# A two-layer hybrid decoder trunk on one core: first rows split in 128-column pieces, first products reordered, last update in halves, transposed rows loaded from ScalarE's queue

## The chip, the cores and the metric

The kernel runs on one core of a Trainium2 chip. The metric is the device time of one execution in microseconds, median of three runs.

## What is computed

A trunk of two layers over 256 tokens of width 1024, all in float32. The reference, cut to its frame:

```python
def hybrid_layer(x, ...):
    proj = rms_norm(x, g_attn_pre) @ w_in + b_in          # 1024 -> 2304: q, k, v of two head groups
    mo = rms_norm(moba_attention(mq, mk, mv), g_moba_out)  # 8 heads; 256 tokens are one block: causal
    so = rms_norm(swa_sink_attention(sq, sk, sv, sinks), g_swa_out)  # window 128, 2 kv heads, sinks
    x = x + rms_norm(concatenate([mo, so]) @ w_out, g_attn_post)
    h = rms_norm(x, g_ffn_pre)
    return x + rms_norm((silu(h @ w_gate) * (h @ w_up)) @ w_down, g_ffn_post)   # d_ff 2816
```

Queries and keys are rotated (rope) before attention.

## The kernel before

**Products.** Each float32 operand is split into a rounded part ("h", made by ScalarE as a copy to float32r) and the residual ("l", made by VectorE as a subtraction), and a product is the sum hh + hl + lh of three TensorE products. The first letter is that of the activations, the second that of the weights. Activations are kept transposed in `actT`, 8 pieces (k) of 128 columns for each of the two row tiles t (128 tokens each).

**Weights.** All weights come as blocks of 128 x 2048 (1 MB), 46 a layer, in the order of use. Block 0 holds 8 k-pieces of 256 columns, blocks 1 and 2 the next 512 columns (4 k each), blocks 3 and 4 the next, and so on. SP issues the load of block b into one of three places of `raw` as soon as VectorE has finished w_l of the block three before it (`load_block`, line 315); ScalarE makes w_h (`hi`, line 502), VectorE w_l (`lo`, line 738), in one of four slots that TensorE frees. `after(L, b)` makes the blocks that the use of block b frees a slot for; in layer 0, after(L, 0) to after(L, 4) make blocks 4 to 8.

**Order.** Every engine's instructions stand in a list written out by hand, once for each engine, and wait on semaphores. TensorE multiplies (`multiply`, line 1087) with the attention steps laid between the blocks: `qk` transposes rotated queries and keys, `scores`, `probs_transposed` (line 1127) takes the exponentials back, `values` (line 1177). VectorE does `project` (bias and rstd, then rope: lines 805 to 835), `maxima` (line 854), `normalise`, `scale_o`, `loT` (line 775: the residual of transposed rows). ScalarE does the exponentials (`exps`, line 568), copies from PSUM (`keep_qk`, line 556) and the sums of squares (`sum_x`, line 537); GpSimd turns those into rstd.

**Start.** The first rows are not transposed on the chip. The host gives x transposed, [128, 8 k, 128 tokens] for each t, and the gains transposed, [128, 8]. SP issues, in this order: xT[0], gT, the first half of block 0, xT[1], the second half, blocks 1 and 2, bias, tables, x (lines 333 to 346). VectorE multiplies xT[0] by the gains (`scale_early`, line 758), GpSimd xT[1] (`scale_first`, line 435), in two halves each. ScalarE rounds each half (`hiT_early`, line 518), VectorE subtracts (`loT_early`, line 766). Blocks 0 and 1 are rounded in halves too (`hi_early`, line 511, and `lo_early`, line 749). TensorE waits for GpSimd's masks, runs eight products on them (`warm`, line 1120), whose result nobody reads, then block 0 in four groups, (half 0, t 0), (half 0, t 1), (half 1, t 0), (half 1, t 1), each with all of hh, lh, hl (`first_block`, line 1112), then block 1 by halves in `multiply`.

**End.** The last tile's y is in two banks; ScalarE sums squares, GpSimd makes rstd, VectorE adds in one instruction of 1024 columns (`update_x`, line 904), and SP stores 512 KB (line 388).

## Time and profile before

| | us |
|---|---|
| median of 3 runs (lowest, highest) | 605.18 (604.11, 605.3) |
| profiled execution, time | 606.41 |
| profiled execution, span | 604.6 |
| TensorE busy | 585.8 (97%) |
| VectorE busy | 361.4 (60%) |
| ScalarE busy | 290.4 (48%) |

The profile is one execution; its span runs from the first to the last instruction. "PE" is TensorE's products, "PEld" its weight loads, DVE VectorE, ACT ScalarE, POOL GpSimd, SPq the DMA queue of SyncE. Ends of products are modelled, so that a row of several products is read by the distance of their starts. The page gives the span in 40 slices of 15.1 us, with the TensorE clock that was granted in each, in tenths. Square brackets behind a row tell how long the engine had been idle before it and what released it.

### The profile page before, as it was taken

The page shows a single profiled execution, that of the slowest core. Times are in us where ns is not written, and L with a number is a line of the kernel's source. Part 1 is how long each engine was busy: PE and PEld are TensorE (multiplying, and loading weights), DVE is VectorE, ACT ScalarE, POOL GpSimd, SP SyncE. Part 2 cuts the span into 40 slices and gives each one's busy share as a digit, 9 for nine tenths or more (in the row PEclk, how much of TensorE's full clock was granted, in tenths as well). Part 3 has the DMA queues.
Part 4 walks back from the last instruction along what each step waited for, and adds up shares of the span by engine and source line. Part 5 has one row for each costly group of instructions (what it writes and reads, how often), then busy time and mean ns, then how long its engine had stood idle before and what let it go on. Part 6 is the DMA issues. An engine that isn't in the chain of part 4 may idle for free.

```text
span 604.6 us, 7614 instructions
## 1 busy us (share of the span) xinstructions
PE 585.8 (97%) x2996; PEld 487.4 (81%) x2996; DVE 361.4 (60%) x458; ACT 290.4 (48%) x406; POOL 45.1 (7%) x70
## 2 busy tenths in 40 slices
PE   5999899999999999999999999999999999999995
PEld 3878787888888889888887788778888888898884
DVE  3878874757545545354596987648556446433632
ACT  3656555746354354155364755466644444423520
POOL 3100000420000000000120010025000000000000
PEclk8899999999999999999999999999999999999999
DMA  8854443157655451549355532416565545342701
GB/s 293 324 197 158 157 181 132 65 215 244 220 198 202 149 207 69 209 151 342 125 208 193 192 132 95 179 66 238 188 241 202 209 150 199 139 178 101 277 1 69
DMA packets 18291, 107.26 MB, mean 177 GB/s; under 512 B 2896, under 2 KB 3152, under 8 KB 6608
## 3 DMA queue, kind: packets, MB, share of 16 engines
q1 hardware_dynamic: 18256, 106.78, 48.0%
q8 instruction: 24, 0.39, 0.2%
q14 instruction: 11, 0.09, 0.0%
HBM read 105.72 MB, written 1.05 MB: 177 GB/s over the span
## 4 chain that ended last, share of the span: by engine, by line
PE 79%; DVE 11%; ACT 6%; issue 2%; DMA 1%; SPq 0%; POOLq 0%; POOL 0%; DVEq 0%; ACTq 0%
PE bank L1087 71%; PE bank L1127 4%; DVE w_l L738 4%; ACT work L568 3%; DVE bank L854 3%; PE bank L1177 2%; ACT w_h L502 2%; PE bank L1112 2%; DMA raw<-in_w_blocks 1%; PE bank L1152 1%; DVE actT_l L775 1%; DVE top L854 1%; DVE work L807 1%; ACT actT_h L530 1%; DVE work L829 1%
## 5 line engine op out<-in xcount | busy, mean ns | idle before, releaser
L738 DVE TENSOR_TENSOR w_l<-raw,w_h 128x2048 fp32r<-128x2048 f32 x90 | 205.5, 2290 | 144.3 <-ACT w_h L502 144.2
L502 ACT ACTIVATE w_h<-raw 128x2048 fp32r<-128x2048 f32 x90 | 171.9, 1916 | 138.0 <-PE bank L1087 119.1
L1087 PE MATMUL bank<-w_h,actT_h 128*128 128x512 f32 (+1 forms) x608 | 235.6, 387 | 1.2 <-DVE actT_l L775 1.0
L1087 PE MATMUL bank<-w_h,actT_l 128*128 128x512 f32 (+1 forms) x608 | 228.9, 377 | 0.0
L1087 PE MATMUL bank<-w_l,actT_h 128*128 128x512 f32 (+1 forms) x608 | 228.3, 375 | 0.0
L1087 PEld LDWEIGHTS bank<-w_h,actT_h 128*128 128x128 f32 x608 | 114.6, 188 | 24.2 <-DVE actT_l L775 3.1
L1087 PEld LDWEIGHTS bank<-w_h,actT_l 128*128 128x128 f32 x608 | 114.4, 188 | 21.5
L1087 PEld LDWEIGHTS bank<-w_l,actT_h 128*128 128x128 f32 x608 | 114.8, 189 | 18.4
L1127 PE MATMUL bank<-ident,work 128*128 128x128 f32 x316 | 46.6, 274 | 4.0 <-ACT work L568 3.3
L1087 PE MATMUL bank<-w_h,fT_h 128*128 128x512 f32 x160 | 49.8, 392 | 0.0
L1087 PE MATMUL bank<-w_l,fT_h 128*128 128x512 f32 x160 | 49.4, 390 | 0.0
L1087 PE MATMUL bank<-w_h,fT_l 128*128 128x512 f32 x160 | 49.3, 389 | 0.0
L1127 PEld LDWEIGHTS bank<-ident,work 128*128 128x128 f32 x316 | 37.3, 141 | 13.6 <-ACT work L568 6.5
L568 ACT ACTIVATE work<-bank,neg_max 128x128 f32<-128x128 f32 (+1 forms) x64 | 26.0, 425 | 36.9 <-DVE neg_max L858 36.9
L1087 PEld LDWEIGHTS bank<-w_l,fT_h 128*128 128x128 f32 x160 | 30.0, 188 | 6.4
L1087 PEld LDWEIGHTS bank<-w_h,fT_l 128*128 128x128 f32 x160 | 30.0, 188 | 6.3
L1087 PEld LDWEIGHTS bank<-w_h,fT_h 128*128 128x128 f32 x160 | 29.5, 188 | 5.7
L449 POOL TENSOR_TENSOR norms<-norms,constants 128x1 f32<-128x1 f32 x8 | 6.7, 840 | 346.6 <-ACT work L546 346.6
L775 DVE TENSOR_TENSOR actT_l<-bank,actT_h 128x512 fp32r<-128x512 f32 (+1 forms) x24 | 14.9, 643 | 23.2 <-ACT actT_h L530 23.2
L606 ACT ACTIVATE work<-bank,norms 128x512 f32<-128x512 f32 (+1 forms) x24 | 15.4, 652 | 22.2 <-PE bank L1087 22.2
L530 ACT ACTIVATE actT_h<-bank 128x512 fp32r<-128x512 f32 (+1 forms) x24 | 12.9, 563 | 27.3 <-PE bank L1127 27.0
L897 DVE TENSOR_TENSOR work<-bank,gain_b 128x512 f32<-128x512 f32 x16 | 10.6, 687 | 24.0 <-ACT work L546 24.0
(73 smaller groups left out, 372.3 us busy)
## 6 DMA issues: line engine op xcount, KB each, us to landing
raw<-in_w_blocks SPq DMA_DIRECT2D x91, 1024.0 KB, 4.8
bias<-in_b_in SPq DMA_DIRECT2D x8, 256.0 KB, 6.2
work<-in_x_transposed SPq DMA_DIRECT2D x2, 512.0 KB, 5.9
raw<-in_w_blocks SPq DMA_DIRECT2D x2, 512.0 KB, 8.6
x<-in_x SPq DMA_DIRECT2D x2, 512.0 KB, 11.3
gain_b<-in_g_attn_post SPq DMA_DIRECT2D x2, 512.0 KB, 7.0
bias<-in_g_ffn_pre SPq DMA_DIRECT2D x2, 512.0 KB, 5.5
gain_b<-in_g_ffn_post SPq DMA_DIRECT2D x2, 512.0 KB, 5.7
```

Of the source, the lines that this page charges most:

```text
L502: nc.scalar.activation(w["h"][:, slot(b), :], raw[:, r, :], ACT.Copy).then_inc(hi_ready, 1)
L530: nc.scalar.activation(dst["h"][:, k:k + nk, tokens(t)], bank[b][:, 0:nk * P].rearrange("p (k n) -> p k n", k=nk), ACT.Copy).then_inc(hiT_ ...
L568: last = nc.scalar.activation(probs[:, j, n * keys:(n + 1) * keys], bank[4 + j][:, n * keys:(n + 1) * keys], ACT.Exp, bias=neg_max[:, g, t ...
L606: nc.scalar.activation(silu[t][:, 0:n], bank[b][:, 0:n], ACT.Silu, scale=rstd_x[:, t:t + 1]).then_inc(drained[b], 1)
L738: nc.vector.tensor_tensor(w["l"][:, slot(b), :], raw[:, slot(b, RAW), :], w["h"][:, slot(b), :].bitcast(F32), ALU.subtract).then_inc(lo_re ...
L775: nc.vector.tensor_tensor(dst["l"][:, k:k + nk, tokens(t)], bank[b][:, 0:nk * P].rearrange("p (k n) -> p k n", k=nk), dst["h"][:, k:k + nk ...
L854: ins = nc.vector.tensor_tensor_reduce(own, own, mask, SCALE, sinks[:, j, head:head + 1] if g == SWA else NEG, ALU.add, ALU.max, top[:, j, ...
L897: nc.vector.tensor_tensor(y[t][:, c, :], bank[b][:], gain_b[:, c * BANK:(c + 1) * BANK], ALU.mult).then_inc(drained[b], 1)
L1087: ins = nc.tensor.matmul(bank[BANK_OF[name]][:, 0:n], left[s][:, at + k, tokens(t)], right[r][:, k, c * BANK:c * BANK + n], start=first an ...
L1112: ins = nc.tensor.matmul(bank[BANK_OF[name]][:, 0:n], actT[s][:, k, tokens(t)], right[r][:, k, :], start=k == 0 and (s, r) == ("h", "h"), ...
L1127: ins = nc.tensor.transpose(out_[:, q * P:(q + 1) * P], src(q), ident[:])
L1177: ins = nc.tensor.matmul(bank[b][:, h * HEAD:(h + 1) * HEAD], probsT[:, j, at:at + P], v[g][:, kb, cols], start=kb == 0, stop=kb == blocks ...
```

## The change

It has eight parts.

1. The transposed rows are loaded by two DMAs on ScalarE's queue; the gains are put in front of the first rows by the host, 1032 columns in one DMA. SP's queue starts with the first half of block 0.
2. The rows are no longer multiplied by the gains beforehand. ScalarE rounds 128 columns at a time with the gain as its scale, VectorE multiplies and subtracts in one instruction of 128 columns. VectorE's, GpSimd's and the halved instructions for them go.
3. ScalarE and VectorE take the first half of block 0 before the second half of the first rows; block 1 is made in one piece instead of two.
4. TensorE runs 16 warming products instead of 8, on a zero tile that VectorE clears, before GpSimd's constants are waited for.
5. TensorE's first products have a new order; in block 1 hh of both tiles, then lh, then hl.
6. In layer 0, ScalarE makes w_h of block 6 before the first exponentials, and VectorE makes w_l of block 7 after `maxima(SWA, 2)` instead of before `project(3, 0)`.
7. In layer 1, VectorE does the residual of the second rows before `project(1, 0)`.
8. The last update is two instructions of 512 columns, each followed by its own store of 256 KB.

The diff, cut to its core (of the old code only what has no counterpart is left out, its functions being described above):

```diff
         y = [work[:, 0:2, :], work[:, 4:6, :]]
...
-        gT = sb("gT", [P, D // P])
+        work_row = work[:].rearrange("p a n -> p (a n)")
+        xT_row = [work_row[:, 4 * BANK - D // P:4 * BANK + D], work_row[:, 4 * BANK + D:4 * BANK + 2 * D]]
...
+        gT = work_row[:, 4 * BANK - D // P:4 * BANK]
+        still = work[:, 9, :].bitcast(BF16)
...
-            sp.dma_start(xT[0], xT_in[0]).then_inc(xT_in_done[0], 16)
-            sp.dma_start(gT[:], gT_in).then_inc(gT_in_done, 16)
             load_first(0)
-            sp.dma_start(xT[1], xT_in[1]).then_inc(xT_in_done[1], 16)
             load_first(1)
...
+            sp.wait_ge(x_ready, X_READY.done(depth - 1, (1, 0)))
+            sp.dma_start(out[0, tokens(0), :], x[:, 0, :]).then_inc(out_done, 16)
+            for c in range(2):
+                sp.wait_ge(half_ready, c + 1)
+                cols = slice(c * BANK, (c + 1) * BANK)
+                sp.dma_start(out[0, tokens(1), cols], x[:, 1, cols]).then_inc(out_done, 16)
...
-            pool.wait_ge(gT_in_done, 16)
-            pool.wait_ge(xT_in_done[1], 16)
-            scale_first(1)
...
-                act.wait_ge(xT_scaled[t], half + 1)
-                k = slice(4 * half, 4 * half + 4)
-                nc.scalar.activation(actT["h"][:, k, tokens(t)], xT[t][:, k, :], ACT.Copy).then_inc(hiT_first[t], 1)
+                if half == 0:
+                    act.wait_ge(xT_in_done[t], 16)
+                for k in range(4 * half, 4 * half + 4):
+                    nc.scalar.activation(actT["h"][:, k, tokens(t)], xT[t][:, k, :], ACT.Copy, scale=gT[:, k:k + 1]
+                                         ).then_inc(hiT_first[t], 1)
...
+            nc.scalar.dma_start(xT_row[0], xT_first_in).then_inc(xT_in_done[0], 16)
+            nc.scalar.dma_start(xT_row[1], xT_second_in).then_inc(xT_in_done[1], 16)
             hiT_early(0, 0)
+            hi_early(0)
             hiT_early(0, 1)
-            hi_early(0, 0)
             hiT_early(1, 0)
-            hi_early(0, 1)
+            hi_early(1)
             hiT_early(1, 1)
-            hi_early(1, 0)
-            hi_early(1, 1)
+            hi(0, 1, wait=False)
             hi(0, 2, wait=False)
...
                     after(L, 1)
+                    after(L, 2)
...
                 keep_probsT(L, SWA, 0)
-                if L == 0:
-                    after(L, 2)
                 after(L, 3)
...
+                for k in range(4 * half, 4 * half + 4):
+                    dve.wait_ge(hiT_first[t], k + 1)
+                    nc.vector.scalar_tensor_tensor(actT["l"][:, k, tokens(t)], xT[t][:, k, :], gT[:, k:k + 1],
+                                                   actT["h"][:, k, tokens(t)].bitcast(F32), ALU.mult, ALU.subtract
+                                                   ).then_inc(loT_first[t], 1)
...
+                for c in range(2):
+                    cols = slice(c * BANK, (c + 1) * BANK)
+                    nc.vector.scalar_tensor_tensor(x[:, 1, cols], y[1][:, c, :], rstd_y[:, 1:2], x[:, 1, cols],
+                                                   ALU.mult, ALU.add).then_inc(half_ready, 1)
...
-            scale_early(0)
+            nc.vector.memset(still, 0.0).then_inc(still_ready, 1)
+            dve.wait_ge(xT_in_done[0], 16)
             loT_early(0, 0)
+            lo_early(0)
             loT_early(0, 1)
-            lo_early(0, 0)
+            dve.wait_ge(xT_in_done[1], 16)
             loT_early(1, 0)
-            lo_early(0, 1)
+            lo_early(1)
             loT_early(1, 1)
-            lo_early(1, 0)
-            lo_early(1, 1)
+            lo(0, 1)
             lo(0, 2)
...
                     lo(L, 3)
-                    project(L, 1, 0)
                     loT(L, ("ht", 0, 1, 0))
                     loT(L, ("ht", 0, 1, 1))
+                    project(L, 1, 0)
                     project(L, 0, 1)
...
                 project(L, 2, 1)
-                after(L, 3)
+                if L:
+                    after(L, 3)
                 project(L, 3, 0)
                 maxima(L, SWA, 2)
+                if L == 0:
+                    after(L, 3)
                 scale_o(L, SWA, 0)
...
+            def early(b, t, half, *parts, last=False):
...
+                for s, r in parts:
+                    pe.wait_ge(lo_half if r == "l" and (b, half) == (0, 0) else
+                               hi_half if (b, half) == (0, 0) else
+                               lo_ready if r == "l" else hi_ready, 1 if (b, half) == (0, 0) else b + 1)
+                    for k in ks:
...
+                        pe.wait_ge((loT_first if s == "l" else hiT_first)[t], k + 1)
...
+                pe.wait_ge(still_ready, 1)
                 for _ in range(n):
-                    nc.tensor.matmul(bank[5][:], masks[:, 1, :], masks[:].rearrange("p a n -> p (a n)"),
-                                     start=True, stop=True)
+                    nc.tensor.matmul(bank[5][:], still[:, 0:P], still[:, P:P + BANK], start=True, stop=True)
...
+            warm(16)
+            early(0, 0, 0, hh, lh, hl)
+            early(0, 1, 0, hh, hl, lh)
+            early(0, 0, 1, hh, lh)
+            early(0, 0, 1, hl, last=True).then_inc(full[BANK_OF["proj", 0, 0]], 1)
+            early(0, 1, 1, hh, hl)
+            early(0, 1, 1, lh, last=True).then_inc(full[BANK_OF["proj", 0, 1]], 1)
+            early(1, 0, 0, hh)
+            early(1, 1, 0, hh)
+            early(1, 0, 0, lh)
+            early(1, 1, 0, lh)
+            early(1, 0, 0, hl)
+            early(1, 1, 0, hl).then_inc(block_used, 1)
+            USED.tick(1)
             pe.wait_ge(const_ready, 8)
-            warm(8)
-            for half in range(2):
-                for t in range(T):
-                    first_block(t, half)
             for L in range(depth):
                 if L == 0:
-                    for half in range(2):
-                        for t in range(T):
-                            multiply(L, t, 1, (half,))
                     multiply(L, 0, 2)
```

## Rows read from the trace of the kernel before

**Rows 1.** The page: TensorE's busy time, share, products; its clock in 40 slices.
```profile
PE 585.8 (97%) x2996; PEld 487.4 (81%) x2996; DVE 361.4 (60%) x458; ACT 290.4 (48%) x406; POOL 45.1 (7%) x70
PEclk8899999999999999999999999999999999999999
```

**Rows 2.** Waits of TensorE over the span: for whom, us in total, times, longest.
```profile
PE bank L1127 <- ACT work L568: 3.3, 6, 1.4
...
PE bank L1087 <- DVE actT_l L775: 1.0, 1, 1.0
```

**Rows 3.** Chain of the work that ended last, 0 to 34 us: start, us, what.
```profile
0.74 0.38 SPq L335
...
1.65 7.78 DMA raw<-in_w_blocks
...
9.45 1.06 ACT w_h L511
...
13.43 6.85 PE bank L1112 x36
20.28 13.63 PE bank L1087 x60
```

**Rows 4.** Stretches: busy and count by engine, granted clock, DMA share, GB/s.
```profile
12.00:18.00 6.00, 5.68 (x25) 5.42 (x26) 4.54 (x5) 4.96 (x6) 1.67 (x2) 0.50 1.01 383
18.00:21.00 3.00, 3.00 (x21) 2.87 (x20) 2.42 (x2) 2.88 (x4) 0.93 (x1) 0.89 0.98 365
```

**Rows 5.** Timeline, 4 to 35 us: start, us, engine, line, what [idle before, releaser].
```profile
4.12 1.42 DVE L758 TENSOR_TENSOR work<-work,gT 128x512 f32<-128x512 f32 x2 [4.12 <-DMA gT<-in_g_first_transposed]
...
4.89 1.32 ACT L518 ACTIVATE actT_h<-work 128x512 fp32r<-128x512 f32 x2 [2.87 <-DVE work L758]
...
5.06 3.54 PE L1120 MATMUL bank<-masks 128*128 128x512 bf16 x8 [5.06 <-POOL masks L419]
...
10.65 0.71 PE L1112 MATMUL bank<-w_h,actT_h 128*128 128x256 f32 x4 [2.05 <-ACT w_h L511]
...
18.85 1.05 ACT L537 ACTIVATE work<-x 128x1024 bf16<-128x1024 f32 x1
...
22.06 0.35 DVE L805 SCALAR_TENSOR_TENSOR v_swa<-bank,norms,bias 128x128 f32<-128x128 f32 x1 [0.79 <-POOL norms L443]
...
25.25 2.28 DVE L738 TENSOR_TENSOR w_l<-raw,w_h 128x2048 fp32r<-128x2048 f32 x1
...
34.06 0.28 ACT L556 ACTIVATE kT<-bank 128x128 f32<-128x128 f32 x1 [5.91 <-PE bank L1127]
```

**Rows 6.** Timeline at layer 0's first maxima and exponentials.
```profile
37.73 0.36 DVE L854 CUSTOM_DVE_ANT_0 bank<-bank,masks,sinks 128x128 f32<-128x128 f32 x1 [4.10 <-PE bank L1152]
...
40.29 0.37 ACT L568 ACTIVATE work<-bank,neg_max 128x128 f32<-128x128 f32 x1 [2.75 <-DVE neg_max L858]
```

**Rows 7.** Timeline of layer 0, w_l of block 7 and TensorE at the third exponentials.
```profile
57.76 2.28 DVE L738 TENSOR_TENSOR w_l<-raw,w_h 128x2048 fp32r<-128x2048 f32 x1
...
65.98 0.63 PE L1127 MATMUL bank<-ident,work 128*128 128x128 f32 x4 [1.43 <-ACT work L568]
66.90 0.30 PE L1127 MATMUL bank<-ident,work 128*128 128x128 f32 x1 [0.28 <-ACT work L568]
```

**Rows 8.** Timeline of layer 1, second rows.
```profile
316.48 0.75 DVE L807 SCALAR_TENSOR_TENSOR work<-bank,norms,bias 128x512 f32<-128x512 f32 x1
...
319.27 1.28 DVE L775 TENSOR_TENSOR actT_l<-bank,actT_h 128x512 fp32r<-128x512 f32 x2
...
320.65 0.36 PE L1087 MATMUL bank<-w_h,actT_h 128*128 128x256 f32 x1 [1.02 <-DVE actT_l L775]
```

**Rows 9.** Timeline of the tail.
```profile
600.28 1.28 DVE L904 SCALAR_TENSOR_TENSOR x<-work,norms,x 128x1024 f32<-128x1024 f32 x1 [0.34 <-POOL norms L452]
601.59 0.34 SPq L388 DMA_DIRECT2D out<-x  x1
```

## What the change does to the time, predicted

> **What bounds the kernel now.** I read the profile page: engine shares, then slices. TensorE is busy 97% of the span of 604.6 us, and only the first two slices have its clock below full [rows 1]. So the reader should look for TensorE's dead time and for the stretch at the low clock. TensorE's own waits, totalled over the span, hold few entries behind the first products: 3.3 us on the exponentials (ScalarE) and 1.0 on actT_l (VectorE) [rows 2]. The change touches the start, three of these waits, and the tail.
>
> The chain of the start [rows 3]: the first half of weight block 0 lands 7.78 us after its issue, at 9.43; ScalarE rounds it in 1.06; TensorE's products of block 0 (line 1112, 48 of them) run to 20.28, and from there on it is fed, 60 products of 512 columns in 13.63 us, 0.2275 each. The 48 have half as many columns, 0.114 each by that row, 5.5 us in all; they take 9.6, from 10.65 on [rows 5], because the granted clock is 0.50 (the 1.2 GHz level) from 12 to 18 us and back near full by 21 [rows 4]. Ahead of the fall TensorE had idled 2.05 us between its eight warming products, 3.54 us from 5.06, and the first real one [rows 5].
>
> **The start: when blocks 0 and 1 can be done.** The warming products no longer wait for GpSimd's masks (5.06) but for a zero tile that VectorE clears. No memset of VectorE is in this trace; a pass of its own over 512 columns is 0.71 (two in 1.42 [rows 5]), and with that they start by 1.5 us. Eight took 3.54, 0.44 each, so sixteen end at 8.5 at the low clock and at 6.5 if it rises half way. They cover the wait for weights and cost nothing on the path; if the weights came first, they would cost what is left of them, 1 us at most.
> The transposed rows leave SP's queue: raw's first half is issued at 0.74, not 1.65 [rows 3]. ScalarE issues the rows instead, two DMAs of 0.38 if priced as SP's [rows 3], beside or ahead of its table load; it did nothing for data until 4.89 [rows 5], so both are covered. When does the half land? At the latest as now, 9.4. At the soonest like the first rows, which with the gains were there at 4.12 [rows 5], plus 1.4 for 512 KB of rows that share the way (383 GB/s [rows 4]): 5.5. I take 7.0, nearer to the soonest, because only 1.4 of the 7.78 us is transfer, and it was issued behind two others.
> What the rows show is that the half lands 5 us behind rows issued 0.9 sooner. The Trainium skill, "DMA: Bandwidth & Descriptors" (Issuing engines are not separate DMA queues), says that DMAs of several engines run on the same 16 DMA engines and that a second issuer saves only issue time. It speaks against this edit: by it the half would land 0.9 us sooner, near 8.5; the sum would stay, as it goes by the cap below, and rival A would grow.
> Pieces: VectorE's scalar_tensor_tensor of 128 columns takes 0.35 [rows 5], so 16 need at most 5.6 us, against four subtractions and two multiplications of 0.71, 4.3: between 0 (they overlap) and +1.3. ScalarE's two halves take 1.32, a copy of 128 columns 0.28 [rows 5]: 16 need 4.5 against 2.6, +1.9, of which half lies ahead of the weights. With the half at 7.0, ScalarE has w_h's half at 8.1, the second rows rounded by 10.3, the rest of block 0 by 11.4 and block 1, two halves of 1.06 [rows 3] from about 14, at 16. VectorE follows by 2.3 for a block (2.28 [rows 5]): block 1's residual at 18.4. TensorE: block 0 needs 5.5 us of full clock and is fed from 8.3 to 14.5; block 1's 16 products that need no residual of w start at 16 and last 3.6, its other 8 last 1.8: done at 21.4, where it is done at 20.28 + 24 x 0.2275 = 25.7 now. 4.3 us sooner.
> **What that is worth.** Behind it stands block 3. Its w_l ends at 27.53, behind two projections on VectorE that begin at 22.06, when rstd is there, 3.2 us after ScalarE's sum_x began at 18.85, when x had landed [rows 5]. Nothing of that chain is edited; it moves only with the backlog of DMAs. TensorE reaches block 3 at 20.28 + 48 x 0.2275 = 31.2 now. So the lead is capped at 31.2 - 27.5 = 3.7 us plus what the backlog gains, at least 0 and at most 1.5 (the first rows had latency and transfer in 3.4 us, 0.74 to 4.12 [rows 3, 5]; with 1.4 of sharing, 3.0 of the 7.78 are stall, and half of it could go). I take 0.3: 4.0 us; bounds at full clock 3.5 and 5.0.
> Later feeding moves along with the lead: VectorE had waited 4.10 us for the scores at 37.73 and ScalarE 2.75 for the maxima at 40.29 [rows 6]. Hoisting after(0, 2) puts one rounding of 1.9 us into the latter wait; behind it are queued the first exponentials, for which TensorE waits. The cover is 0.8 us; each us beyond it costs one.
>
> **Layer 0, w_l of block 7 behind the maxima.** Its 2.28 us at 57.76 stand in VectorE's run ahead of the maxima; TensorE waits 1.43 at 65.98 and 0.28 at 66.90 for the exponentials that need them [rows 7]. Taken out, the maxima come 2.28 sooner, more than the 1.71, and what is late next is TensorE's own order. The moved instruction ends when VectorE's next step began before, so nobody behind it is later; the next raw load, which waits for it, goes out 4.7 us later (60.04 to about 64.8), between 0 and 1 us. I take 1.6 of the 1.71.
> **Layer 1, loT ahead of project(1, 0).** TensorE waits 1.02 at 320.65 for actT_l, whose two halves (1.28) run from 319.27, behind a projection that began at 316.48 [rows 8]. Swapped, loT is through by 318, TensorE wants it at 319.6: the wait goes, and the projection, ending 1.3 later at 320.6, is wanted by a transpose behind six products of 0.2275 and eight shorter. 1.0.
> **Tail.** Now one update of 1.28 and one DMA of 512 KB, from 601.59 to the end at 604.63 [rows 9]. In halves: two updates of 0.7, one DMA beside the second, and the last moves 256 KB: 0.7 less at 383 GB/s, 0.15 more to compute. Bounds 0 and 0.7; 0.5.
>
> **The sum:** 4.0 + 1.6 + 1.0 + 0.5 = 7.1 us. On the profiled execution: span 604.6 to 597.5, time 606.4 to 599.3. The median of the runs, 605.18, lies 1.2 below the profiled one: 598.1.
>
> **Rivals.**
> Low clock at the start (A). If the half lands late, TensorE idles over 2 us behind the warming products, as it did ahead of the fall [rows 4, 5]; a second pause stands ahead of block 1 (14.5 to 16). Against it: the pause of 1.43 at 65.98 lies in slices whose clock is full [rows 1, 7]. If it falls as now, for some 7 us, half of them, 3.4, is lost; 1.0 of that is slack ahead of block 3, so the lead is 1.6: 600.5. Here a rule speaks for the forecast: the Trainium skill, "TensorE: Matmul & The Clock Gate" (What's actually happening and its table), has the clock fall only after a whole idle window. The fall in [rows 4] came with 2.05 us of idling, so I go by the row.
> The reorders return nothing (B): from 66 us on VectorE and ScalarE pace the attention steps, TensorE's waits there are small [rows 2], and what is won ahead of it is lost there: without the 1.6 and 0.5 of the lead, 600.2.
> The backlog gains more (C): 5.0 or over, 597.1 and below.
> It does not do what it says (D): weights as late as now and the clock down, so only layer 1 and the tail pay: 603.7.
> Slower (E): the clock stays at 1.2 GHz through block 1, because TensorE now runs small groups released piece by piece, as from 12 to 18 us, where its busy time of 5.68 in 6.00 [rows 4] did not lift it. The three blocks up to block 3 are 16.4 us of work at full clock from 8.3 on; low until T, they end at 8.3 + 16.4 + (T - 8.3)/2. Low until block 1 is done, T = 30, block 3 is reached at 35.6 instead of 31.2: 4.4 us lost against 3.1 won elsewhere, 606.5. It decides from T = 27.5.
>
> **How the numbers follow.** Forecast 0.54 (597.1 to 599.4), A 0.17, B 0.13, C 0.08, D 0.05, E 0.03. The range 596.0 to 602.0 leaves out D, E and part of C and of A, 0.15. A measurement of this kernel can tell about 0.2%, 1.2 us: faster by more holds in all but E and part of D, 0.93; same 0.04; slower 0.03.
>
> **What would show it.** Right: the first L511 between 5.5 and 8, block 1's last product near 21.4, w_l of block 3 ending near 27 and TensorE on block 3 right behind; no wait of TensorE on ScalarE near 62 and on L775 near 312; a last DMA of 256 KB 2.4 us before the end; granted clock 1.00 from 8 us on. Wrong: a clock of 0.50 behind 8 us (A, E), the first exponentials late behind the hoisted rounding, new waits between 62 and 105 us (B), or the half at 9 us again.

## The result and the profile after

| | us |
|---|---|
| before, median of 5 runs beside the changed kernel (lowest, highest) | 604.11 (602.63, 605.3) |
| after, median of 5 (lowest, highest) | 598.48 (598.25, 598.82) |
| ratio, with its 95% interval | 0.9907 [0.9886, 0.9928] |
| profiled execution of after: time, span | 598.48, 596.7 |

The changed kernel is 5.6 us faster by the medians. Between the two profiled executions the distance is larger, 604.6 to 596.7, 7.9 us. That difference is the main thing to be explained.

The page of after, its sections 1 and 2: busy time of TensorE, and the clock in 40 slices. [rows 1] show the low slices at the start, which are gone.

```profile
PE 585.4 (98%) x3004; PEld 486.1 (81%) x3004; DVE 362.0 (61%) x469; ACT 292.8 (49%) x417; POOL 42.1 (7%) x68
...
PEclk9999999999999999999999999999999999999999
```

The waits of TensorE over the whole span of after (us in total, times, longest):

```profile
PE bank L1108 <- ACT w_h L500: 1.6, 1, 1.6
PE bank L1123 <- ACT work L559: 1.5, 4, 0.8
PE bank L1117 <- DVE work L912: 1.5, 1, 1.5
PE bank L1123 <- ACT kT L547: 0.5, 1, 0.5
```

Against [rows 2] the wait on the exponentials fell from 3.3 to 1.5, the 1.0 on actT_l is gone, and the wait for w_h between the warming products and the first real one is 1.6 where it was 2.1.

The chain of waits of after in its first 36 us (start, us, what), from the DMA to the feeding of blocks 0 to 3:

```profile
0.74 6.18 DMA work<-in_x_first_transposed
6.94 1.28 ACT actT_h L508 x4
8.22 0.96 ACT w_h L500
9.22 1.22 PE bank L1108 x8
10.48 10.94 PE bank L1108 x64
21.42 8.16 PE bank L1083 x36
```

Compare [rows 3]. The chain no longer begins with the weights but with the first rows, which land 6.18 us after their issue; ScalarE's four pieces (0.32 each) come next, and only then the first half of block 0, which had landed by then: 6.0 us after its issue at 0.74. TensorE is fed without a gap from 10.48.

The timeline of after, rows of TensorE, ScalarE and VectorE (start, us, engine, line, operation; idle time before it and its releaser in brackets):

```profile
1.45 6.17 PE L1117 MATMUL bank<-work 128*128 128x512 bf16 x16 [1.45 <-DVE work L912]
...
8.13 1.04 ACT L500 ACTIVATE w_h<-raw 128x1024 fp32r<-128x1024 f32 x1
...
9.22 0.74 PE L1108 MATMUL bank<-w_h,actT_h 128*128 128x256 f32 x4 [1.60 <-ACT w_h L500]
...
15.79 2.00 PE L1108 MATMUL bank<-w_h,actT_h 128*128 128x512 f32 x8
...
24.04 2.29 DVE L729 TENSOR_TENSOR w_l<-raw,w_h 128x2048 fp32r<-128x2048 f32 x1
```

And its windows of the same stretches as [rows 4] (busy time of each engine, granted clock, DMA share, GB/s): the clock is 1.00 where it was 0.50 and 0.89.

```profile
12.00:18.00 6.00, 6.00 (x42) 5.55 (x41) 5.30 (x10) 5.26 (x7) 0.00 (x0) 1.00 1.03 327
18.00:21.00 3.00, 3.00 (x15) 2.49 (x14) 2.23 (x2) 2.31 (x4) 1.13 (x3) 1.00 0.85 338
```

The end of after in its timeline, beside [rows 9]: the last piece of 512 columns begins at 593.44, its store is issued at 594.21, and the span ends 2.5 us later, at 596.7.

```profile
593.44 0.75 DVE L897 SCALAR_TENSOR_TENSOR x<-work,norms,x 128x512 f32<-128x512 f32 x1
594.21 0.33 SPq L391 DMA_DIRECT2D out<-x  x1
```

**Where the 7.9 us lie.** A mark that both profiles have is the first transpose of `qk(0, 0)`, behind block 3: it begins at 33.75 before and at 29.43 after, 4.3 us for the start. From there to the seam of the layers the two profiles differ by 1.95 (layer 0's reorder), in layer 1 by 1.26, from the last product on by 0.43 (tail). Together 7.96. For layer 1 the timeline of after has the residual of the rows, which ended the wait in [rows 8], already at 310.71, ahead of the projection that stood before it:

```profile
310.71 1.29 DVE L756 TENSOR_TENSOR actT_l<-bank,actT_h 128x512 fp32r<-128x512 f32 x2 [0.40 <-ACT actT_h L521]
311.91 0.74 DVE L788 SCALAR_TENSOR_TENSOR work<-bank,norms,bias 128x512 f32<-128x512 f32 x1
```

### The profile page after: what moved, and what is told of

Its sections match the earlier page's. It is cut to its first block, busy times and chain, and to the rows that moved or that the text cites. A ratio compares the mean times of both kernels' runs of the same rounds, so it can differ in the third digit from the quotient of the medians.

```text
span 596.7 us, 7657 instructions
## 1 busy us (share of the span) xinstructions
PE 585.4 (98%) x3004; PEld 486.1 (81%) x3004; DVE 362.0 (61%) x469; ACT 292.8 (49%) x417; POOL 42.1 (7%) x68
## 4 chain that ended last, share of the span: by engine, by line
PE 85%; DVE 6%; ACT 6%; DMA 1%; issue 1%; DVEq 0%; POOLq 0%; POOL 0%; ACTq 0%
PE bank L1083 75%; PE bank L1123 4%; ACT work L559 3%; DVE w_l L729 3%; PE bank L1173 2%; DVE bank L835 2%; PE bank L1108 2%; ACT w_h L494 2%; PE bank L1148 1%; DMA work<-in_x_first_transposed 1%; DVE actT_l L756 1%; DVE top L835 0%; ACT actT_h L521 0%; ACT work L575 0%; DVE neg_max L839 0%
## 5 line engine op out<-in xcount | busy, mean ns | idle before, releaser
L729 DVE TENSOR_TENSOR w_l<-raw,w_h 128x2048 fp32r<-128x2048 f32 x91 | 207.7, 2290 | 144.2 <-ACT w_h L494 144.1
L494 ACT ACTIVATE w_h<-raw 128x2048 fp32r<-128x2048 f32 x91 | 173.9, 1917 | 143.0 <-PE bank L1083 118.1
L1083 PE MATMUL bank<-w_h,actT_h 128*128 128x512 f32 (+1 forms) x600 | 232.3, 387 | 0.2
L1083 PE MATMUL bank<-w_h,actT_l 128*128 128x512 f32 (+1 forms) x600 | 225.9, 377 | 0.0
L1083 PE MATMUL bank<-w_l,actT_h 128*128 128x512 f32 (+1 forms) x600 | 225.2, 375 | 0.0
L1083 PEld LDWEIGHTS bank<-w_h,actT_h 128*128 128x128 f32 x600 | 113.1, 189 | 22.6 <-issue 2.7
L1083 PEld LDWEIGHTS bank<-w_h,actT_l 128*128 128x128 f32 x600 | 112.9, 188 | 21.2
L1083 PEld LDWEIGHTS bank<-w_l,actT_h 128*128 128x128 f32 x600 | 113.2, 189 | 18.3
```

What stands on the lines that cost most here:

```text
L494: nc.scalar.activation(w["h"][:, slot(b), :], raw[:, r, :], ACT.Copy).then_inc(hi_ready, 1)
L729: nc.vector.tensor_tensor(w["l"][:, slot(b), :], raw[:, slot(b, RAW), :], w["h"][:, slot(b), :].bitcast(F32), ALU.subtract).then_inc(lo_re ...
L1083: ins = nc.tensor.matmul(bank[BANK_OF[name]][:, 0:n], left[s][:, at + k, tokens(t)], right[r][:, k, c * BANK:c * BANK + n], start=first an ...
```

## The experiments

The theory was that every part pays as in the sum of the prediction. The rivals to be told apart: whether the start gives its 4.0 us in the usual execution or only against the profiled one, and which of its edits gives it: warming, clock, queue, pieces, order of products, or the gains that stop having a DMA of their own. The batches ran on several chips, and the kernel before, repeated beside each, had medians of 603.76 (18 runs), 605.31 (12), 605.56 (10) and 605.5 (11), with single runs from 601.76 to 606.34. So each ratio is taken against the runs beside it. Where two medians of different batches are compared below, that is said. Kernels whose start does not vary agree across the batches to 0.2 us (598.45, 598.57, 598.6), so the chips themselves hardly differ; it is the start of before that does. "Mark" below is the start of that first transpose in the profile of the kernel.

**1. Parts 6 to 8 alone** (`b_678`: the kernel before with only the reorders and the tail)

```diff
+                    after(L, 2)
                 ...
-                if L == 0:
-                    after(L, 2)
...
-                    project(L, 1, 0)
                     loT(L, ("ht", 0, 1, 0))
                     loT(L, ("ht", 0, 1, 1))
+                    project(L, 1, 0)
```

> The kernel before with parts 6, 7 and 8 alone: w_h of block 6 and w_l of block 7 moved in layer 0, the second rows' residual ahead of project(1, 0) in layer 1, the last update and store in halves. Start as before. My sum gives 1.6 + 1.0 + 0.5 = 3.1 us. If the attention stage eats the reorders (rival B): 1.5 us. In the trace: no wait of TensorE of 1.43 near 64 us and none of 1.02 near 319 us. Theory 'the first lead makes them larger' (they pay only with TensorE ahead): under 2.5 us here, against the 3.4 that the two profiles differ by behind 34 us.

600.03 (598.74 to 601.85, 7 runs) against 603.76: 3.7 us, ratio 0.9937 [0.9913, 0.996]. Its start is unedited, and yet its profile has the mark at 29.73, not 33.75, and a full clock: in this execution the first half of the weights landed 5.7 us after its issue at 1.64, not 7.78. Its timeline, the first w_h:

```profile
7.34 1.06 ACT L515 ACTIVATE w_h<-raw 128x1024 fp32r<-128x1024 f32 x1 [0.98 <-DMA raw<-in_w_blocks]
```

So the start of [rows 3 to 5] is not what the unchanged code always does. It is one outcome of several, and this profile is one too: with 598.74 it is of the fastest of the seven runs.

The mean granted clock, which is on record for each single run, tells how often. Before's profile, with its fall of some 7 us, has 0.992. Of the 51 runs of before in these batches 16 have 0.992 or 0.993, with a median of 606.0 us; 12 have 0.994 or 0.995 (605.5 us); 23 have 0.996 or more (603.8 us). The share differs by batch: 5 of 18 runs at 0.995 or below where the median was 603.76, and 23 of 33 in the other three.

**2. Parts 1 to 5 alone** (`a_no678`: after with 6, 7 and 8 put back)

> The changed kernel with parts 6, 7 and 8 undone: only the start is changed (rows on ScalarE's queue, pieces, order, warming). Theory 'luck' (the start of before varies from execution to execution by where the weights land and whether the clock falls; the profiled one was a slow one, so the start is worth less on the median than the 4.3 us between the two profiles): the median gains 1.5 to 2 us over before, though its profile reaches the first transposes near 29.4 us. Theory 'sum' (my 4.0 us for the start): the median gains 4 us.

601.96 (601.69 to 603.56, 7 runs), ratio 0.9954 [0.9935, 0.9973]: 3.5 us slower than after, so parts 6 to 8 are worth 3.7 added and 3.5 taken away. The waits of TensorE in this kernel show the two terms coming back, 2.9 for 1.5 on the exponentials and the 1.0 on actT_l:

```profile
PE bank L1104 <- ACT work L555: 2.9, 7, 0.8
...
PE bank L1064 <- DVE actT_l L753: 1.0, 1, 1.0
```

What is left for the start is 600.03 - 598.48 = 1.5 us by the medians of two batches on top of parts 6 to 8 (1.6 within the batch of `b_678`, against `a_sp_rows` of experiment 5). By the runs beside this kernel it is more: 605.31 - 601.96 = 3.4 by the medians, 2.8 by the ratio (0.46%), which has an interval of 1.6 to 3.9. The batches differ in how often before has its slow start, and the worth of the start with them.

**3. The clock alone** (`b_warm34`: before, with 34 warming products on a zero tile in place of 8)

```diff
+            warm(34)
             pe.wait_ge(const_ready, 8)
-            warm(8)
```

> The kernel before with one edit: 34 warming products on a zero tile cleared by VectorE instead of 8 on the masks, so that TensorE is busy up to about 10.5 us; rows, pieces, order and queues stay as they were. Theory 'clock' (most of what the start gained is that TensorE's clock no longer falls; the earlier rows and weights and the new order bring little): granted clock 1.00 throughout, block 2 is started near 21.5 (bound by w_l of block 2, which ended at 21.3 in before) instead of 25.6, block 3 near 27.5, and the time falls by 3.0 to 3.7 us. Theory 'feeding' (the start gained because rows and weights are ready sooner and are used in a better order): the old order with its waits for whole halves starves TensorE whatever its clock, block 2 starts at 24 or later, gain under 1.5 us.

604.12 (603.43 to 605.67, 12 runs), ratio 1.0002 [0.9987, 1.0018]: nothing on the median. In its profile the clock never fell, though the half again landed 8.0 us after its issue; of its 12 runs two have a mean clock of 0.994 and 0.995. Its timeline, the warming products and the first w_h:

```profile
1.45 10.09 PE L1124 MATMUL bank<-work 128*128 128x512 bf16 x34 [1.45 <-DVE work L922]
...
9.62 1.06 ACT L513 ACTIVATE w_h<-raw 128x1024 fp32r<-128x1024 f32 x1 [3.26 <-DMA raw<-in_w_blocks]
```

And its window, with a clock of 1.00 where [rows 4] have 0.50:

```profile
12.00:18.00 6.00, 5.24 (x43) 4.86 (x41) 4.38 (x5) 4.85 (x6) 1.83 (x2) 1.00 1.03 376
```

Between its profile and that of before the mark moved from 33.75 to 31.99: between these two executions, a clock that stays up is worth 1.8 us. The run tells less about the median than meant, because 34 were too many: the first real product began at 11.19, 0.5 us after its weights were ready at 10.68. In an execution with the early half, as in the profile of `b_678` (weights ready at 8.40), the same warming would stand in the way for 2.8 us, by an estimate from these two rows.

**4. Half the warming in the changed kernel** (`a_warm8`: `warm(8)` for `warm(16)`)

> The changed kernel with 8 warming products instead of 16 (nothing else). They end near 5 us, TensorE idles 4 us until the first weights at 9.2. Theory 'clock': the granted clock falls to 0.50 from some point before 12 us, block 0 and part of block 1 run at half speed, the time rises by 2 to 4 us over the changed kernel. Theory 'feeding': no more than 0.5 us, since nothing is fed later.

599.56 (598.97 to 599.93, 6 runs), ratio 0.9927: 1.1 us slower than after, and the ranges don't touch. TensorE idled 4.0 us, and the clock fell for a short time (0.50 from 8.7 to 12.1 us). Its timeline, the first real product, and then its window from 6 to 12 us, where the mean clock is 0.72:

```profile
9.06 1.22 PE L1108 MATMUL bank<-w_h,actT_h 128*128 128x256 f32 x4 [4.01 <-ACT w_h L500]
```

```profile
6.00:12.00 6.00, 2.94 (x14) 2.94 (x14) 4.10 (x12) 5.22 (x14) 0.00 (x0) 0.72 1.03 430
```

So the longer warming is worth about 1 us here on the median. In the profile it is less: the mark is at 29.87 for 29.43. That eight are enough where the rows come from SP's queue (experiment 7) suggests that the longer warming only pays for the later landing of the rows; that was not shown by a run of its own.

**5. The rows on SP's queue again** (`a_sp_rows`: after, gains still merged, rows issued by SP in the old order)

```diff
+            sp.dma_start(xT_row[0], xT_first_in).then_inc(xT_in_done[0], 16)
             load_first(0)
+            sp.dma_start(xT_row[1], xT_second_in).then_inc(xT_in_done[1], 16)
             load_first(1)
...
-            nc.scalar.dma_start(xT_row[0], xT_first_in).then_inc(xT_in_done[0], 16)
-            nc.scalar.dma_start(xT_row[1], xT_second_in).then_inc(xT_in_done[1], 16)
```

> The changed kernel with the two loads of transposed rows back on SP's queue in the old order (rows, first half of block 0, second rows, second half), nothing on ScalarE's queue. If the second queue matters: the first half lands 1 us or more later than in the changed kernel (there before 8.1), ScalarE's first rounding of weights starts later and block 1 ends later; +0.5 to +1.5 us, or more if the longer idling lowers the clock. If a second issuer only saves issue time: rows land sooner (near 4 us), the half near 8.5, no more than 0.5 us either way, since block 3 (VectorE's w_l) caps the lead.

598.45 (597.92 to 599.28, 6 runs), ratio 0.991 [0.9884, 0.9937]: the same as after. The queue is worth nothing. The half of the weights lands 5.9 us after its issue at 1.18, at 7.03, against 6.0 after 0.74 in after: the second issuer saved 0.3 us. The rows now land 3.3 us after their issue, where they took 6.18 on ScalarE's queue, and w_h starts 1.1 us sooner, at 7.05, on the weights. Most of that is lost again at block 3, as [rows 5] had let expect: VectorE's w_l is not done in time, and TensorE waits for it (mark at 28.99, 0.4 sooner than after). Three rows of its timeline:

```profile
7.05 1.06 ACT L502 ACTIVATE w_h<-raw 128x1024 fp32r<-128x1024 f32 x1 [1.76 <-DMA raw<-in_w_blocks]
...
23.79 2.29 DVE L729 TENSOR_TENSOR w_l<-raw,w_h 128x2048 fp32r<-128x2048 f32 x1 [0.25 <-ACT w_h L496]
...
26.13 0.50 PE L1083 MATMUL bank<-w_h,actT_h 128*128 128x512 f32 x1 [0.33 <-DVE w_l L729]
```

**6. Halves for pieces** (`a_halves`: after with the first rows rounded and subtracted in instructions of 512 columns. It leaves out the multiplication of the first rows by the gains)

```diff
-                for k in range(4 * half, 4 * half + 4):
-                    nc.scalar.activation(actT["h"][:, k, tokens(t)], xT[t][:, k, :], ACT.Copy, scale=gT[:, k:k + 1]
-                                         ).then_inc(hiT_first[t], 1)
+                k = slice(4 * half, 4 * half + 4)
+                nc.scalar.activation(actT["h"][:, k, tokens(t)], xT[t][:, k, :], ACT.Copy).then_inc(hiT_first[t], 1)
```

> The changed kernel with the first rows handled in halves of 512 columns (4 instructions on ScalarE and 4 on VectorE instead of 16 and 16). It leaves out the multiplication of the first rows by their gains, since one instruction can take only one gain per partition. Price of the pieces alone: ScalarE spends 2.5 us on them instead of 5.0, VectorE 2.8 instead of 4.5. Theory 'capped' (block 3 and the DMA backlog set the lead): same time within 0.3 us. If the pieces are on the path: 0.5 to 1 us faster.

598.6 (597.81 to 599.01, 6 runs), ratio 0.9897 [0.9875, 0.9919]: the same as after. Here w_h starts at 7.14, 1.0 sooner: 0.65 by the pieces (0.54 us from the first rounding to w_h, for 1.19 in after), the rest because the rows landed 0.3 sooner in this execution. Again TensorE waits at block 3, by the view of its waits:

```profile
PE bank L1082 <- DVE w_l L728: 0.2, 1, 0.2
```

Two kernels whose first products come a microsecond earlier (8.16 and 8.23 against 9.22) have their marks only 0.4 and 0.7 earlier (28.99 and 28.77), and on the median they end together with after: the cap at block 3 holds.

**7. Parts 6 to 8 with the gains merged** (`b_678_merged`: `b_678`, and the gains stand in front of the first rows in one DMA; order, queue, halves, eight warming products and the order of the products as before)

```diff
-            sp.dma_start(xT[0], xT_in[0]).then_inc(xT_in_done[0], 16)
-            sp.dma_start(gT[:], gT_in).then_inc(gT_in_done, 16)
+            sp.dma_start(xT_row[0], xT_first_in).then_inc(xT_in_done[0], 16)
             load_first(0)
-            sp.dma_start(xT[1], xT_in[1]).then_inc(xT_in_done[1], 16)
+            sp.dma_start(xT_row[1], xT_second_in).then_inc(xT_in_done[1], 16)
             load_first(1)
```

> The kernel before with parts 6, 7 and 8 and the gains in front of the first rows in one DMA (of the start nothing else: SP's queue in the old order, two multiplications on VectorE and two on GpSimd, halves, 8 warming products on the masks). Theory 'gains' (the 128 rows of 32 bytes queued ahead of the first half of block 0 stall some of the DMA engines: in the kernels that have that DMA the half took 5.7, 7.3, 7.8 and 8.0 us, in those without it 5.7 to 6.0): the half takes 6 us or less, the median falls from 600.0 to about 599, and the spread shrinks. Theory 'accident' (late landings come from somewhere else): median 599.7 to 600.7, the half at 7 us or more in the profile as likely as not.

598.57 (598.16 to 598.67, 4 runs), ratio 0.9884 [0.9871, 0.9898]. That is the time of after, without the other queue, the pieces, the longer warming and the new order. Against `b_678`, in another batch, the one edit takes 1.5 us by the medians and 3.2 by the two ratios (0.9884 for 0.9937), and the spread goes from 3.1 us (7 runs) to 0.5 (4 runs). The half lands 6.0 us after its issue; the first w_h in the timeline:

```profile
7.17 1.06 ACT L515 ACTIVATE w_h<-raw 128x1024 fp32r<-128x1024 f32 x1 [0.93 <-DMA raw<-in_w_blocks]
```

Its chain of waits runs elsewhere, over the second rows and GpSimd's multiplication of them, and so does that of `b_678` in its profile:

```profile
1.63 6.83 DMA work<-in_x_second_transposed
...
8.63 1.77 POOL work L439
...
11.99 4.10 PE bank L1130 x32
```

From there TensorE is fed, and the mark is at 29.56 (after: 29.43). That chain leaves slack for the first products, which fits with more warming bringing nothing to this start, as the next two runs find.

**8 and 9. Sixteen warming products with either form of the gains** (`b_678_warm16`, `b_678_merged_w16`: on the zero tile, ahead of the wait for the constants)

```diff
+            warm(16)
             pe.wait_ge(const_ready, 8)
-            warm(8)
```

> The kernel before with parts 6, 7 and 8 and the 16 warming products on a zero tile, started by VectorE's clearing; rows, pieces, order and queues as before. If warming is what the start is worth on the median: 598.5 to 599, as the changed kernel, and less spread than b_678 (598.7 to 601.9). If the order and the pieces matter: 599.5 to 600, as b_678 without it (600.03).

> As b_678_merged, and with the 16 warming products on VectorE's zero tile. With the weights sooner the products end less than 2 us ahead of the first real one: the granted clock stays up in every run. If landing and clock together are what the start is worth, 598.5 to 598.8 as the changed kernel. If the new order and the dropped multiplications are worth something of their own, it stays at 599.2 or above.

600.67 (599.31 to 602.6, 6 runs), ratio 0.9932, with the gains apart; 598.68 (598.54 to 599.09, 4 runs), ratio 0.9889, with the gains merged. Warming changes neither (ratios 0.9937 and 0.9884 without it); merging is again worth 2.0 us by the medians and 2.6 by the ratios, in two batches. The first of the two caught a late landing in its profile, 7.3 us after issue, an idle time of 3.46, and the fall of the clock. Its timeline, the first w_h and the first real product, then its window from 12 to 18 us (clock 0.76):

```profile
8.91 1.06 ACT L517 ACTIVATE w_h<-raw 128x1024 fp32r<-128x1024 f32 x1 [2.56 <-DMA raw<-in_w_blocks]
...
10.11 0.71 PE L1134 MATMUL bank<-w_h,actT_h 128*128 128x256 f32 x4 [3.46 <-ACT w_h L517]
```

```profile
12.00:18.00 6.00, 5.56 (x38) 5.30 (x37) 4.95 (x5) 5.49 (x6) 1.12 (x2) 0.76 1.05 357
```

Over the profiles of this study the half lands 7.78, 5.7, 8.0 and 7.3 us after its issue where the gains' DMA stands ahead of it on its queue (before, `b_678`, `b_warm34`, `b_678_warm16`), and 5.9 to 6.0 where it does not (`a_sp_rows`, `b_678_merged`, `b_678_merged_w16`). In the seven profiles in which the half is first on SP's queue it is 5.4 to 6.0. The second rows, which follow the half on that queue, show the same: 8.6, 6.7, 8.7 and 8.1 us with the gains' DMA, 6.7 to 6.9 without.

**10 and 11. The gains apart, behind the rows on ScalarE's queue** (`a_gain_apart`: after, with a DMA of 128 rows of 32 bytes for them; `a_gain_wide`: the same with rows of 512 bytes)

```diff
             nc.scalar.dma_start(xT_row[0], xT_first_in).then_inc(xT_in_done[0], 16)
+            nc.scalar.dma_start(gT, gT_in).then_inc(gT_in_done, 16)
             nc.scalar.dma_start(xT_row[1], xT_second_in).then_inc(xT_in_done[1], 16)
...
                     act.wait_ge(xT_in_done[t], 16)
+                    if t == 0:
+                        act.wait_ge(gT_in_done, 16)
```

> The changed kernel with the gains in a DMA of their own (128 rows of 32 bytes) behind the first rows on ScalarE's queue, nothing else. Theory 'gains': the first half of block 0 or the second rows land 1 to 2 us later in some runs, median 599 to 600, spread over 1 us. Theory 'accident': 598.3 to 598.7, as the changed kernel.

> This is a_gain_apart with one difference: the gains, still in a DMA of their own behind the first rows on ScalarE's queue, come as 128 rows of 512 bytes (64 KB, padded with zeros) instead of 128 rows of 32 bytes (4 KB). Sixteen times as many bytes, and the same number of DMAs in the same order. If it is the rows of 32 bytes that hold up what lies beside them, the delay goes: the time is that of after, 598.5 us (597.9 to 599.2), the first w_h of block 0 starts near 8 us in the profile instead of 10.56, and the granted clock stays up. If it is the further DMA, or the further semaphore that ScalarE and VectorE wait for, whatever its rows are, nothing changes: 602.0 us (601.4 to 602.8), w_h again at 10 us or later. Between them, about 600, would mean that both carry a share.

602.03 (601.72 to 603.01, 5 runs), ratio 0.9943, and 602.99 (602.0 to 603.4, 6 runs), ratio 0.9958. The whole gain of the start is gone in both, and the size of the rows is not the cause. The chain of waits of `a_gain_apart` says what is:

```profile
1.17 6.84 DMA work<-in_g_first_transposed
...
8.09 1.28 ACT L511
...
9.38 1.28 ACT actT_h L511 x4
10.66 0.96 ACT w_h L501
```

The gains land 6.84 us after their issue, although they are 4 KB, and ScalarE can go on at 8.09, where the rows let it begin at 6.94 in after. The 1.28 at 8.09 is ScalarE's table load: with a second wait ahead of the first rounding it stands behind the wait, where in after it lay hidden at 1.66. 1.15 + 1.28 = 2.4 us, and w_h starts at 10.56 for 8.13. TensorE then idles 3.7 us, the clock falls (0.53 from 12 to 18 us), and the mark is at 33.74 for 29.43: 4.3 us, of which 2.4 are the later w_h; the other 1.9 are put down to the clock.

The table load in the timeline of after, and then in that of `a_gain_apart`:

```profile
1.66 1.28 ACT L508 ACT_TABLE_LOAD   x1 [1.66 <-PEq L1371]
```

```profile
8.09 1.28 ACT L511 ACT_TABLE_LOAD   x1 [8.09 <-DMA work<-in_g_first_transposed]
```

The half of the weights itself landed 5.4 and 5.5 us after its issue in the two, so on another queue this DMA does not hold it up. But it does hold up what stands behind it on its own queue, the second rows. Their time from issue to landing in after, `a_gain_apart` and `a_gain_wide`, each from the view of the line that issues them (L601, L605, L606):

```profile
DMA to landing us min/median/max: 8.6/8.6/8.6
DMA to landing us min/median/max: 10.1/10.1/10.1
DMA to landing us min/median/max: 10.3/10.3/10.3
```

In the four other kernels that have both rows on ScalarE's queue without this DMA it is 8.2 to 8.4. Rows of 512 bytes delay them as much as rows of 32, so the small rows are not needed for a delay of this size.

**12. TensorE's own order** (`a_plus`: after, and products moved between dependent steps)

```diff
-                    multiply(L, 0, 3)
+                    multiply(L, 0, 3, (0,))
                     qk(L, 0, 0)
+                    multiply(L, 0, 3, (1,))
...
                     probs_transposed(L, SWA, 0, 0)
-                    probs_transposed(L, SWA, 0, 1)
                     multiply(L, 1, 4, (0,))
+                    probs_transposed(L, SWA, 0, 1)
...
                 probs_transposed(L, MOBA, 2, 0)
-                probs_transposed(L, MOBA, 2, 1)
                 multiply(L, 0, 12, (0,))
+                probs_transposed(L, MOBA, 2, 1)
```

> The changed kernel with TensorE's order edited at the waits that are left: qk(0, 0) of layer 0 between the halves of block 3, half a block between the two probs_transposed of the first round (layer 0) and of the last MOBA round (both layers). The waits there are 0.45, 0.76, 0.28 and 0.28 us. If they are dead time of TensorE alone, 1.7 us less: 596.7. If VectorE or ScalarE pace these stages, the waits appear elsewhere: under 0.8 us.

596.61 (596.44 to 596.97, 5 runs), ratio to before 0.9866 [0.9845, 0.9888], 1.9 us faster than after (2.0 than `a_halves`, the same as after, in its own batch): the fastest kernel here. The 0.5 on kT is gone, and of the 1.5 on the exponentials 0.5 is left, by its waits:

```profile
PE bank L1123 <- ACT work L559: 0.5, 2, 0.3
```

## Why the prediction was right, and where it was not

**The time.** 598.1 was forecast and 598.48 measured, inside the likeliest case. But the gain was 5.6 us, not the 7.1 of the sum: the three runs of before shown ahead of the prediction had a median of 605.18, and with two more beside them it is 604.11. How large the gain is depends on which runs of before one takes. Over all 56 on record before has 605.1, which makes it 6.6; `a_sp_rows`, as fast as after, gains 5.3 in its batch and `b_678_merged` 7.0 in its own. So the time agrees partly by luck: a start valued too high was taken from a median of three that could as well have been 1 us lower.

**The start: 4.0 forecast, 4.3 between the profiles, 1.5 to 3.4 on the medians.** From block 1 on the mechanism inside the profile went as told: block 1's last product at 15.79 + 24 x 0.2275 = 21.25, forecast 21.4; w_l of block 3 done at 26.33, TensorE on block 3 at about 26.7, and no wait between. The first link did not: w_h of the first half began at 8.13 and was done at 9.17, where the sum had it done at 8.1 and the list of signs had it begin between 5.5 and 8. It waited not for the weights but for the first rows, which landed at 6.92 and not near 4 as in before, and for four pieces of them. The slack ahead of block 3 hid that. The cap was tested from the other side by `a_sp_rows` and `a_halves`, which reach it with 0.3 and 0.2 us of waiting. (The bounds told for this term, 3.5 and 5.0, do not come out of its own figures: 3.7 and between 0 and 1.5 more make 3.7 and 5.2.) The step that failed is the one that carried the sum over to the median: "The median of the runs, 605.18, lies 1.2 below the profiled one". It shifts the time by 1.2 and leaves the term of the start at its size in that one execution, an execution with the late half (7.78 us) and the low clock. `b_678` shows that the same code also lands it in 5.7 with the granted clock at 1.00. The late landing and the fall of the clock are outcomes that vary between executions of before. By an estimate from the runs sorted by their clock, with 3.6 us for parts 6 to 8 and 598.5 for after, the start is worth 606.0 - 3.6 - 598.5 = 3.9 us in executions with the low clock of the profile, as forecast, and 603.8 - 3.6 - 598.5 = 1.7 in those with 0.996 or more. A large part of what the change does for the start is to remove that variation: after spreads over 0.6 us, before over 2.7.

**When the half lands.** 7.0 was taken for the time of its landing, and it landed at 6.7; in after it isn't on the chain, the rows are. The argument "only 1.4 of the 7.78 us is transfer, and it was issued behind two others" had the right suspect in its second half, one of the two others: the gains' DMA, if not the reason. But the gain was put down to the queue, and `a_sp_rows` shows that the queue is worth 0. Here the rule of the Trainium skill that was cited against the edit ("DMA: Bandwidth & Descriptors", Issuing engines are not separate DMA queues) was right: 598.45 against 598.48. The rows even came later by it: 6.18 us from issue, issued beside the weights, for 3.3 when SP issued them ahead of the weights.

**Warming and clock.** Forecast: covered, and worth something only if it prevents the fall. The sixteen took 6.17 us and ended at 7.6, between the 6.5 and the 8.5 of the prediction. After idles 1.6 us and keeps its clock; with eight products it idles 4.0 and loses it for 3.4 us, 1.1 us on the median. Rival A did not come, but its mechanism is real and near: `a_warm8` and `a_gain_apart` are it. Idling over 2 us, its condition, does not settle it: `a_plus` idled 2.02 us at this place and kept a clock of 1.00, before lost it with 2.05. Rivals C (a start worth 5.0 or more) and E (the clock low through block 1) did not come either.

**Pieces.** Forecast between 0 and +1.3 us on VectorE and +1.9 on ScalarE, half of it ahead of the weights. Measured: with pieces of 0.32 w_h starts 0.65 us later behind the first rounding than with halves (1.19 for 0.54), and the cap hides it.

**Layer 0: 1.6 forecast, 1.95 between the profiles**, of which 1.8 stand in the waits (3.3 to 1.5). The rounding hoisted ahead of the exponentials delayed nobody. **Layer 1: 1.0 forecast**, the wait of 1.0 is gone; between the profiles 1.26. **Tail: 0.5 forecast, 0.43 measured.** Together 3.1 forecast, 3.7 and 3.5 measured by adding and by taking away. Rival B, that they return nothing, is ruled out. So is D, by the ratios of both halves. The other edits of the start (queue, pieces, warming, order of products, block 1 in one piece) bring nothing together over merging that these runs can tell from 0: `b_678_merged` has none of them and takes 598.57. The order and block 1 were not run alone.

**What stays open.** Why a DMA of 4 KB in 128 rows of 32 bytes, between the rows and the weights on one queue, makes the half land up to 2 us later in some executions and not in others (5.7 us in `b_678`). On ScalarE's queue a DMA with rows of 512 bytes at that place delays what follows it as much as one with rows of 32, which speaks for the further DMA and against its small rows; on SP's queue the two were not told apart. That the late landing behind the gains' DMA is their doing rests on four profiles against ten, and on the medians of the two merged kernels. How often before's executions have the late half is known only by way of their clock (28 of 51 at 0.995 or below), and a late half need not bring the clock down: in the profile of `b_warm34` it did not.

## What to carry to other kernels

A term that is read at the start of one profiled execution, at a low clock or behind a late DMA, is a sample: ask, with the spread of the runs and the mean clock of each, how often it comes, before it is added to a sum for the median. Put small parameters that the first work needs into the DMA that carries its data, not beside it: that alone gave what the other edits of the start were made for. And before an earlier start is polished further, find the next load that caps it; here block 3 took back 0.6 and 0.3 us of the further microsecond that two of the kernels had won in their profiles, and the rest did not show on the median.

## What the runs showed of the hardware that was not expected

- A DMA of 4 KB, queued between larger ones, takes about as long as they do: on ScalarE's queue 6.84 us from issue, behind 512 KB of rows that took 5.6, with 64 KB in its place 7.0; on SP's queue in before 2.8, behind rows that took 3.1. What stood behind it on ScalarE's queue took 10.1 and 10.3 us, for 8.2 to 8.6 without it.
- ScalarE's table load (1.28 us) lies where the instruction list puts it relative to the waits: hidden at 1.66 with one wait ahead of the first rounding, exposed at 8.09 (and 8.27 in `a_gain_wide`) with two.
- TensorE kept a granted clock of 1.00 through idle times of 1.6 us ([rows 7] had 1.43) and of 2.02 in `a_plus`, and fell to 0.50 with idle times of 2.05 [rows 5], 3.46, 3.7, 3.9 and 4.0. In before and `b_678_warm16` it fell over 1 us after the first real product had begun, in the others before it. It stayed at 1.2 GHz for 3.4 us in `a_warm8` and in `b_678_warm16`, and for 6.8 in before, `a_gain_apart` and `a_gain_wide`. The idle time of `a_plus`:

```profile
9.10 0.73 PE L1108 MATMUL bank<-w_h,actT_h 128*128 128x256 f32 x4 [2.02 <-ACT w_h L500]
```

- The granted clock does not tell how fast the first products run. Up to the falls told above it reads 1.00 in all of these profiles, and yet the first warming products of after, 512 columns each, begin 0.43 us apart and the last ones 0.22. In `b_678` and `b_678_merged`, with eight of them, the first real products still begin at twice the distance that they have a microsecond later (0.21 for 0.12).
